# Reordering the stage of the 31-tap convolution: long taps first on VectorE, short convolution within the layer norm, third projection around the norm's steps

## The reference

```python
def even_mixer(h, w_in, sc_conv_w, cf_conv_w, cf_conv_b, cf_ln_g, cf_ln_b, w_out):
    z = h @ w_in
    sc_b, sc_c, sc_x, cf_a, cf_g = jnp.split(
        z, [SC_WIDTH, 2 * SC_WIDTH, 3 * SC_WIDTH, 3 * SC_WIDTH + CF_WIDTH], axis=-1)
    y_sc = sc_b * causal_dwconv_2(sc_c * sc_x, sc_conv_w)
    u = cf_a * jax.nn.sigmoid(cf_g)
    u = causal_dwconv_2(u, cf_conv_w) + cf_conv_b
    u = jax.nn.silu(layernorm(u, cf_ln_g, cf_ln_b))
    return jnp.concatenate([y_sc, u], axis=-1) @ w_out
```

## Time and profile before

| | us |
|---|---|
| median of 3 runs | 2221.65 |
| lowest and highest | 2220.83, 2225.66 |
| profiled execution | 2223.43 |
| its span | 2221.6 |
| TensorE busy | 2065.4 (93%) |
| VectorE busy | 1507.2 (68%) |
| ScalarE busy | 1032.1 (46%) |
| GpSimd busy | 132.0 (6%) |

### The profile page before, as it was taken

The page is one execution under the profiler, slowest core; times in us unless marked ns, Lnnn a source line. Parts: engine busy times, 40 slices in busy tenths (PEclk is TensorE's granted clock), DMA queues, the critical chain, the costliest instruction groups (busy, mean ns, idle before and its releaser), DMA issues.

```text
span 2221.6 us, 40600 instructions
## 1 busy us (share of the span) xinstructions
PE 2065.4 (93%) x15894; PEld 1999.9 (90%) x15894; DVE 1507.2 (68%) x2267; ACT 1032.1 (46%) x1605; POOL 132.0 (6%) x78
## 2 busy tenths in 40 slices
PE   7999999878999999998998799998969999969999
PEld 7999889768999999997987789998969999849999
DVE  6566867557766666677875667656958677676766
ACT  5444543544544544454435344444625454644543
POOL 0000012010000000000310000000600000100000
PEclk9999999989999999999999899998979999969999
DMA  6554532223556555554313244554424554513554
GB/s 223 187 174 153 189 115 76 96 95 105 172 178 181 169 183 176 187 164 142 117 65 105 95 151 153 187 181 157 132 86 159 179 183 157 159 50 114 190 188 133
DMA packets 90964, 328.06 MB, mean 148 GB/s; under 512 B 10224, under 2 KB 11376, under 8 KB 90736
## 3 DMA queue, kind: packets, MB, share of 16 engines
q1 hardware_dynamic: 90288, 324.50, 45.2%
q10 hardware_dynamic: 576, 2.16, 0.3%
HBM read 325.57 MB, written 1.05 MB: 147 GB/s over the span
## 4 chain that ended last, share of the span: by engine, by line
PE 73%; DVE 17%; ACT 4%; DMA 2%; issue 2%; POOL 0%; SPq 0%; ACTq 0%; DVEq 0%
PE ps L1777 72%; DVE w_lo L1008 5%; DMA raw<-stream 2%; ACT w_hi L476 2%; DVE arena L1270 1%; DVE arena L1030 1%; DVE arena L1529 1%; DVE a_lo L1051 1%; PE ps L1952 1%; DVE x L1019 1%; PE ps L2156 1%; POOL sc L924 0%; DVE tmp L1061 0%; DVE arena L1281 0%; DVE arena L1137 0%
## 5 line engine op out<-in xcount | busy, mean ns | idle before, releaser
L1777 PE MATMUL ps<-a_hi,w_hi 128*128 128x256 f32 x4464 | 1283.7, 288 | 36.1 <-DVE a_lo L1051 8.0
L1777 PE MATMUL ps<-a_hi,w_lo 128*128 128x256 f32 x4464 | 1270.4, 285 | 0.0
L1777 PE MATMUL ps<-a_lo,w_hi 128*128 128x256 f32 x4464 | 1262.0, 286 | 0.0
L1777 PEld LDWEIGHTS ps<-a_hi,w_hi 128*128 128x128 f32 x4464 | 868.8, 195 | 45.6 <-issue 19.0
L1008 DVE TENSOR_TENSOR w_lo<-raw,w_hi 128x1024 fp32r<-128x1024 f32 x614 | 753.2, 1233 | 190.7 <-ACT w_hi L476 190.1
L1777 PEld LDWEIGHTS ps<-a_hi,w_lo 128*128 128x128 f32 x4464 | 868.4, 195 | 0.0
L1777 PEld LDWEIGHTS ps<-a_lo,w_hi 128*128 128x128 f32 x4464 | 864.1, 195 | 0.5
L476 ACT ACTIVATE w_hi<-raw 128x1024 fp32r<-128x1024 f32 x614 | 636.2, 1051 | 297.6 <-DMA raw<-stream 169.9
L1071 DVE TENSOR_TENSOR arena<-ps,arena 128x512 f32<-128x512 f32 x132 | 91.1, 690 | 306.2 <-PE ps L1777 306.0
L924 POOL TENSOR_TENSOR sc<-sc,nhalf 128x2 f32<-128x2 f32 (+5 forms) x25 | 60.9, 2440 | 1802.5 <-DVE sc L1035 1317.7
L520 ACT ACTIVATE arena<-arena 128x256 f32<-128x256 f32 x88 | 36.9, 420 | 248.7 <-DVE arena L1071 247.5
(11 more groups left out here) (291 smaller groups left out, 1513.2 us busy)
## 6 DMA issues: line engine op xcount, KB each, us to landing
raw<-stream SPq DMA_DIRECT2D x613, 512.0 KB, 3.7
gates<-late ACTq DMA_DIRECT2D x1, 1088.0 KB, 5.7
out<-x SPq DMA_DIRECT2D x8, 128.0 KB, 2.0
con<-consts SPq DMA_DIRECT2D x1, 800.0 KB, 9.7
raw<-stream ACTq DMA_DIRECT2D x1, 512.0 KB, 3.8
x<-x_in ACTq DMA_DIRECT2D x2, 256.0 KB, 6.2
x<-x_in SPq DMA_DIRECT2D x2, 256.0 KB, 6.0
par<-params SPq DMA_DIRECT2D x1, 451.0 KB, 7.9
```

Of the source, the lines that this page charges most:

```text
L1777: return nc.tensor.matmul(o, a, b, start=start, stop=stop, **k)
```

## The change

Only the order of the stage's instructions and the semaphores between them change; the arithmetic stays.

- VectorE: 7 long taps instead of 5 after each of channels 1 to 3, 4 instead of 3 after each of the eight splits, and the 7 that are left after one more split. The add of GpSimd's part and of the diagonal taps follows at once. The short convolution is cut in two halves of two channels (`short_taps`, `short_out`, `short_low`), the first placed while TensorE forms the sum, the second while it forms the squares' sum and the next units. The splits move with them.
- ScalarE: products for GpSimd begin after channel 1 (2, then 4 and 4 instead of 3 and 3); the last ones come right after the first split behind the loops. `ysc_hi` is cut in two and comes after the squares.
- TensorE: the diagonal taps come right after unit 15, in banks 2 and 3 instead of 4 and 5. Two units of the third projection follow, then the sum over channels (bank 4 instead of 7), the other two units, the sum of squares, unit 8 of `w_out`, the spread (bank 4 instead of 6), and units 9 to 15.

```diff
--- before.py
+++ after.py
...
-DVE2_STEPS = ["ysc_lo", "cf0", "cf1", "cen0", "cen1", "lnvar", "lndiag", "yb0", "yb1", "o2_0", "o2_1", "o2_lo0", "o2_lo1", "lamz", "xc", "sp4", "gin", "dvar0", "dvar1", "dqk", "xin", "m2",
+DVE2_STEPS = ["cf0", "cf1", "cen0", "cen1", "ysc_lo0", "lnvar", "lndiag", "ysc_lo1", "yb0", "yb1", "o2_0", "o2_1", "o2_lo0", "o2_lo1", "lamz", "xc", "sp4", "gin", "dvar0", "dvar1", "dqk", "xin", "m2",
...
-ACT2_STEPS = ["diag0", "diag1", "diag2", "diag3", "ysc_hi", "lnsq0", "lnsq1", "lnth0", "lnth1", "o2_hi0", "o2_hi1", "spe", "lgsq", "gth", "dsq", "rth", "ith", "a", "tq", "dilT", "mult", "ylru_hi"]
+ACT2_STEPS = ["diag0", "diag1", "diag2", "diag3", "lnsq0", "lnsq1", "ysc_hi0", "ysc_hi1", "lnth0", "lnth1", "o2_hi0", "o2_hi1", "spe", "lgsq", "gth", "dsq", "rth", "ith", "a", "tq", "dilT", "mult", "ylru_hi"]
...
-                    if i > 1:
-                        products(3)
-                    else:
+                    products((0, 2, 4, 4)[i])
+                    if i < 2:
                         diagonals(i)
...
-                for i in range(4):
-                    split(n0 + 16 + i + AHEAD)
-                    products(4)
-                act.wait_ge(b_read, 2)
-                nc.scalar.activation(a_hi[:, 8:12, :], o2[:, 0:4, :], ACT.Copy).then_inc(*AC2.sig(0, "ysc_hi"))
-                for k in range(3):
-                    split(POS["ev_out"] + k + AHEAD)
+                b0, e0 = n0 + 16, POS["ev_out"]
+                split(b0 + AHEAD)
+                products(4 * POOL_TAPS)
+                split(b0 + 1 + AHEAD)
                 for p in range(2):
...
-                split(POS["ev_out"] + 3 + AHEAD)
+
+                def ysc_high(q):
+                    act.wait_ge(b_read, q + 1)
+                    nc.scalar.activation(a_hi[:, 8 + 2 * q:10 + 2 * q, :], o2[:, 2 * q:2 * q + 2, :], ACT.Copy).then_inc(*AC2.sig(0, f"ysc_hi{q}"))
+
+                ysc_high(0)
+                split(b0 + 2 + AHEAD); split(b0 + 3 + AHEAD)
+                ysc_high(1)
+                split(e0 + AHEAD); split(e0 + 1 + AHEAD)
                 for p in range(2):
...
+                split(e0 + 2 + AHEAD)
...
-                for k in range(4, 8):
-                    split(POS["ev_out"] + k + AHEAD)
+                for k in range(3, 8):
+                    split(e0 + k + AHEAD)
...
-                step, EARLY, MEAN = 0, 5, 3
...
-                for k in range(SCK):
-                    for i in range(4):
-                        w = whole("scconv", SCK * i + k)
-                        if k == 0:
-                            dve.wait_ge(pair_read, 5 + i)
-                            n[i] = tick(V.tensor_scalar(ysc[:, i, :], cx[:, i, 0:TOK], w, None, ALU.mult))
-                        else:
-                            need(n[i])
-                            n[i] = tick(V.scalar_tensor_tensor(ysc[:, i, :], cx[:, i, k:k + TOK], w, ysc[:, i, :], ALU.mult, ALU.add))
-                for q in range(2):
-                    for i in range(2):
-                        split(n0 + 16 + 2 * q + i + AHEAD)
-                        taps(step, step + MEAN)
-                        step += MEAN
-                    dve.wait_ge(unit_used, n0 + 18 + 2 * q)
+                b0, e0 = n0 + 16, POS["ev_out"]
+
+                def short_taps(q):
+
+                    for k in range(SCK):
+                        for i in (2 * q, 2 * q + 1):
+                            w = whole("scconv", SCK * i + k)
+                            if k == 0:
+                                dve.wait_ge(pair_read, 5 + i)
+                                n[i] = tick(V.tensor_scalar(ysc[:, i, :], cx[:, i, 0:TOK], w, None, ALU.mult))
+                            else:
+                                need(n[i])
+                                n[i] = tick(V.scalar_tensor_tensor(ysc[:, i, :], cx[:, i, k:k + TOK], w, ysc[:, i, :], ALU.mult, ALU.add))
+
+                def short_out(q):
+                    dve.wait_ge(unit_used, b0 + 2 + 2 * q)
                     need(n[2 * q + 1])
                     V.tensor_tensor(flat(o2[:, 2 * q:2 * q + 2, :]), flat(ysc[:, 2 * q:2 * q + 2, :]), bank(6 + q), ALU.mult
                                     ).then_inc(b_read, 1)

-                dve.wait_ge(*AC2.at(0, "ysc_hi"))
-                V.tensor_tensor(a_lo[:, 8:12, :], o2[:, 0:4, :], a_hi[:, 8:12, :], ALU.subtract).then_inc(*DV2.sig(0, "ysc_lo"))
-                split(POS["ev_out"] + AHEAD)
+                def short_low(q):
+                    dve.wait_ge(*AC2.at(0, f"ysc_hi{q}"))
+                    V.tensor_tensor(a_lo[:, 8 + 2 * q:10 + 2 * q, :], o2[:, 2 * q:2 * q + 2, :], a_hi[:, 8 + 2 * q:10 + 2 * q, :],
+                                    ALU.subtract).then_inc(*DV2.sig(0, f"ysc_lo{q}"))
+
+                split(b0 + AHEAD)
                taps(step, 4 * DVE_TAPS)
...
                 dve.wait_ge(part_sum, 4 * POOL_TAPS)
@@ -1580,27 +1588,35 @@
                 dve.wait_ge(*PE2.at(0, "cfps"))
...
                     v = flat(cf[:, 2 * p:2 * p + 2, :])
-                    V.tensor_tensor(v, v, bank(4 + p), ALU.add).then_inc(*DV2.sig(0, f"cf{p}"))
-                split(POS["ev_out"] + 2 + AHEAD)
+                    V.tensor_tensor(v, v, bank(2 + p), ALU.add).then_inc(*DV2.sig(0, f"cf{p}"))
+                short_taps(0)
+                split(b0 + 1 + AHEAD)

                 dve.wait_ge(*PE2.at(0, "mean"))
-                dve.wait_ge(*DV2.at(0, "cf1"))
                 for i in range(4):
-                    e = V.scalar_tensor_tensor(cf[:, i, :], bank(7, 0, TOK), -1.0 / 512, cf[:, i, :], ALU.mult, ALU.add)
+                    e = V.scalar_tensor_tensor(cf[:, i, :], bank(4, 0, TOK), -1.0 / 512, cf[:, i, :], ALU.mult, ALU.add)
...
-                split(POS["ev_out"] + 3 + AHEAD)
+                short_out(0)
+                short_taps(1)
+                split(b0 + 2 + AHEAD)
+                short_low(0)
+                split(b0 + 3 + AHEAD)
                 dve.wait_ge(*PE2.at(0, "lnstat"))
                 V.tensor_scalar(sc[:, 278:280], bank(5, 0, 2), 1.0 / 512, EPS, ALU.mult, ALU.add).then_inc(*DV2.sig(0, "lnvar"))
+                short_out(1)
                 dve.wait_ge(*PO2.at(0, "lnrs"))
                 tick(V.tensor_scalar(diag[:, 0:128], ident, sc[:, 276:277], None, ALU.mult))
                 V.tensor_scalar(diag[:, 128:256], ident, sc[:, 277:278], None, ALU.mult).then_inc(*DV2.sig(0, "lndiag"))
+                split(e0 + AHEAD)
+                short_low(1)
+                split(e0 + 1 + AHEAD)
                 dve.wait_ge(*PE2.at(0, "lnbc"))
...
-                for k in range(4, 8):
+                for k in range(2, 8):
                     split(POS["ev_out"] + k + AHEAD)
...
                 for i in range(4):
-                    fm(n0 + 16 + i, bank(6 + i // 2, (i % 2) * TOK, (i % 2 + 1) * TOK))
-                for i in range(4):
                     pe.wait_ge(*AC2.at(0, f"diag{i}"))
-                    if i == 0:
-                        pe.wait_ge(pair_read, 8)
-                    o = bank(4 + i // 2, (i % 2) * TOK, (i % 2 + 1) * TOK)
+                    pe.wait_ge(pair_read, 4)
+                    o = bank(2 + i // 2, (i % 2) * TOK, (i % 2 + 1) * TOK)
                     for k in range(PE_TAPS):
                         e = mm(o, wdiag[:, PE_TAPS * i + k, :], ub[:, i, DVE_TAPS + k:DVE_TAPS + k + TOK], start=(k == 0),
                                stop=(k == PE_TAPS - 1))
                 e.then_inc(*PE2.sig(0, "cfps"))
-                pe.wait_ge(*DV2.at(0, "ysc_lo"))
-                km(POS["ev_out"], 8, True, False)
+
+                def b_unit(i):
+                    fm(n0 + 16 + i, bank(6 + i // 2, (i % 2) * TOK, (i % 2 + 1) * TOK))
+
+                b_unit(0)
+                b_unit(1)
+                pe.wait_ge(pair_read, 8)
                 for i in range(4):
                     pe.wait_ge(*DV2.at(0, f"cf{i // 2}"))
-                    e = mm(bank(7, 0, TOK), ones[:], cf[:, i, :], start=(i == 0), stop=(i == 3))
+                    e = mm(bank(4, 0, TOK), ones[:], cf[:, i, :], start=(i == 0), stop=(i == 3))
                 e.then_inc(*PE2.sig(0, "mean"))
-                km(POS["ev_out"] + 1, 9, False, False)
+                b_unit(2)
+                b_unit(3)
                 for c in range(4):
                     pe.wait_ge(*AC2.at(0, f"lnsq{c // 2}"))
                     for j in range(TT):
                         e = mm(bank(5, j, j + 1), tmp[:, c, 128 * j:128 * j + 128], ones[:, 0:1], start=(c == 0 and j == 0),
                                stop=(c == 3), skip_group_check=True)
                 e.then_inc(*PE2.sig(0, "lnstat"))
+                pe.wait_ge(*DV2.at(0, "ysc_lo0"))
+                km(POS["ev_out"], 8, True, False)
+                pe.wait_ge(*DV2.at(0, "lndiag"))
+                mm(bank(4, 0, TOK), ones[:], diag[:]).then_inc(*PE2.sig(0, "lnbc"))
+                km(POS["ev_out"] + 1, 9, False, False)
+                pe.wait_ge(*DV2.at(0, "ysc_lo1"))
```

(2 more changed lines are left out.)

4 lines of the change are left out of this document (2 added, 2 removed).

## The result

The changed kernel takes 2200.55 us (median of four runs, 2198.61 to 2201.97). The kernel before, timed beside it, takes 2223.65 us (2220.83 to 2226.19). The ratio is 0.9893, 95% interval 0.9878 to 0.9908: 1.1% faster. The forecast was 2202.5 against a shown median of 2221.65, so the measured time is 2 us under it and inside the forecast's own range. The profiled execution took 2198.61 us.

The account below looks back on a forecast made before the run. VectorE's order, not TensorE's own work, was taken to limit the stage: `cf0` at 1613.4 plus 35.5 us of TensorE work ends it at 1648.9 against 1667.97, so 2221.65 - 19.1 = 2202.5 us; own range 2197 to 2206.5, widened to 2196.5 to 2211.

Parts of the forecast that it names:

- (e): TensorE from `cf0` to the stage's end: its work sums to 35.5 us, ending at 1648.9 against 1667.97, 19.1 less.
- (a): VectorE's first loop: six more long taps and slower work add 3.6 us; second loop starts at 1572.0 instead of 1568.34.
- (b): VectorE's second loop: eight long taps in each of four turns instead of six, ending at 1607.5 us.
- turn 0: First turn of VectorE's second loop: all eight taps slowed beside GpSimd, 10.2 us, to 1582.2.
- turn 1: Second turn of that loop: GpSimd runs out of products while ScalarE awaits a load; 6.8 us, to 1589.0.
- (c): VectorE behind the loops: split, last 7 taps and adds take 5.9 us; `cf0` at 1613.4 instead of 1627.43.
- (d): TensorE ahead of the sum: diagonal taps end at 1599.3; one 8.3 us wait replaces those for `ysc_lo` and the sum.
- (f): Norm behind `cf0`: every VectorE step must meet its slot under TensorE's units; narrowest room 1.0 us, at the diagonals.
- GpSimd beside all of it: Rival: GpSimd adds throughout VectorE's second loop, turns cost 10.7 us, `cf0` at 1620.7; 2209.8 us; chance 0.12.
- A wait comes back: Rival: one norm slot missed by 3.8 us, next unit at half clock, 6.0 us lost; 2208.5 us; chance 0.16.
- Lock step: Rival: TensorE and VectorE alternate without overlap behind `cf0`, 33 us lost; 2235.5 us; chance 0.03.
- not what it says: Rival: diagonal taps or GpSimd's part, not VectorE's taps, release `cf0`, so the gain vanishes; 2221 us; chance 0.02.

Follow-up runs that it names:

- e_short_before: The changed kernel with the 12 short-convolution instructions put back ahead of the last 7 long taps on VectorE; 2206.32 us, ratio 0.9919.
- e_after_again: The changed kernel, unedited, timed and traced a second time on another chip; 2201.18 us, ratio 0.9895 against the kernel before.
- e_b_three_before: The changed kernel with three third-projection units ahead of the sum, one behind, and VectorE's norm order turned for earlier diagonals; 2202.88 us, ratio 0.9905.
- e_b_all_first: The changed kernel with all four third-projection units ahead of the diagonal taps on TensorE; 2203.36 us, ratio 0.9907.
- e_b_before_sum: The changed kernel with all four third-projection units after the diagonal taps and ahead of the sum over channels; 2199.00 us, ratio 0.9892.

## Why the prediction was right, point by point

**The bound.** VectorE's work decides when the sum starts, and the sum's start decides the rest. e_short_before shows the first directly (4.2 us of VectorE ahead of the sum, 4.4 us later), and the part behind the sum was 35.85 us against the 35.5 of step (e).

**(a), (b) The loops.** On the axis of the trace before (2.06 us added) the second loop begins at 1573.0, forecast 1572.0: 1.0 us late. Step (a) took 0.6 us of VectorE's idle time in the first loop to be filled; none was (5.2 us idle, 4.9 before), which is 0.9 of the 1.0. The second loop's turns take 8.3, 7.0, 9.8 and 8.0 us; the forecast had 10.2, 6.8, 10.2 and 8.3. The term that was mis-sized is turn 0. I took GpSimd to add beside all of it; it paused for 2.76 us there (its row above), since ScalarE stood 1.98 us on a load. It is the same mechanism that I used for turn 1, a turn earlier than I had it. The loop ends at 1606.1 on that axis, forecast 1607.5: it gained 1.9 + 0.4 + 0.3, less 0.2, and lost the 1.0. That the two errors, 1.0 late and 2.4 early, partly cancel is luck. In e_after_again, the same kernel, both fall otherwise: 4.1 us idle in the first loop, and turns of 9.9, 6.7, 10.1 and 7.9 us, turn 0 with a pause of GpSimd of only 1.14. Its loop ends 0.35 us sooner after the fixed point than after's. The end of the loops is firmer than their parts.

**(c) `cf0`.** 6.17 us from the loop's end to the sum's start (1604.02 to 1610.19), forecast 5.9. The sum starts at 1612.3 on that axis, forecast 1613.4. The cover that step (d) counted on held: the diagonal taps end at 1597.1 and GpSimd at 1600.8, both long before.

**(d) TensorE.** One wait of 7.33 us, forecast 8.3, and half clock in one stretch around it. None on `ysc_lo`.

**(e), (f) The norm.** Every slot held: TensorE has no wait on squares, diagonals or low halves behind the sum. The room at the squares' sum is even on the other side: VectorE waited 1.54 us for it. 35.85 against 35.5: the clock came back 6.0 us after the sum's start instead of 4.6, and the small multiplies were a little cheaper. One reading of step (f) was wrong. It has the norm's result `o2_lo0` wanted at 26.6 us after `cf0`; but unit 12 follows the spread after three units, not four, so by its own terms that is 14.7 + 0.44 + 3 x 2.88 = 23.8, with 0.8 us of room for a result due at 23, and this was the narrowest room. In the trace `o2_lo0` is there at 23.2 and wanted at 24.2. e_b_three_before missed just this slot, by 0.61 us.

**The sum.** Forecast 19.1 us for the stage, measured 19.9 (144.24 less 124.36), the 0.8 us being the 1.1 at the sum's start less 0.35 behind it. The forecast for the medians was 19.1 too; measured 23.1 between the two medians (21.1 against the median shown before). By e_after_again's trace the stage's gain is 21.5 us. The rest, 3.2 us or 1.6, lies in stages that the change doesn't touch and that wander by as much between two traces of one kernel. So that the forecast median came within 2 us of 2200.55 owes something to the wandering; the 19.1 us for the stage doesn't.

**The rivals.** *GpSimd beside all of it* would have put the sum at 1620.7; it came at 1612.3, as GpSimd paused and ended at 1602.8 on that axis. Its mechanism is real, though: the adds cost 0.40 to 0.46 us each by four kernels, idle time allowed for. The forecast carried that cost in its slowed taps and splits, and didn't ask whether the adds are worth it. *A wait comes back* didn't happen; e_b_all_first and e_b_before_sum show what it looks like when it does, and that it then cost little, since the units that would have filled it had been done earlier. *Lock step* and *not what it says* have nothing for them.

**What the argument over-rated.** The prediction begins with 19.5 us of waits and with units at half clock, as if the filling were half of the matter. The runs give it less. With none of the projection's units in the norm the stage loses 2.1 us where they delay the diagonal taps and wait for splits themselves (e_b_all_first), and nothing where they stand just ahead of the sum (e_b_before_sum); two waits of over 2 us are back in both.

**The rule of the Trainium skill.** Rows gave the taps at twice their time beside the adds. The Trainium skill (GPSIMD Engine Reference, Key points) says that GpSimd contends with VectorE instructions that have two SBUF inputs, and also that VectorE is structurally about twice as fast for elementwise work. The traces agree with both: taps slow down and products with a PSUM operand don't, and an add takes 1.05 us on GpSimd, a whole tap 0.40 on VectorE. The cost of 0.40 to 0.46 us an add, from the runs above, speaks against the nine taps on GpSimd, which the change left as they were, and not against the change.

## What to carry to other kernels

Find the one result that both engines' orders hinge on, and move everything that isn't needed for it behind it; a microsecond so moved was worth nearly a microsecond, while it hardly mattered which of TensorE's waits a unit filled. Before leaving work on GpSimd beside a busy VectorE, cut it to one column and see what VectorE gains: here each fp32 add of 256 columns cost VectorE about as much as doing the tap itself. When comparing such kernels, take off the idle time that VectorE gained or lost. Judge such an edit by the stage between two fixed points of the trace, as the rest of the program wandered by more than the edit was worth.
